# ScalarE's split of the next weight piece moved to the front of its half step

## The reference

```python
# layer 0
h = rms_norm(x, even_norm_g[i]);  proj = h @ even_w_in[i]         # q, k, v, z_a, u, z_b
q, k = rms_norm(q heads), rms_norm(k heads)                        # 8 heads of 128
o_a = stick_breaking_attention(q, k, v) * silu(z_a)                # exp(log_beta + rest)
o_b = s5_mixer(u, ...) * silu(z_b)                                 # state space, gelu, GLU
x = x + concatenate([o_a, o_b]) @ even_w_out[i]
# layer 1
proj = rms_norm(x, odd_norm_g[i]) @ odd_w_in[i]                    # q, k, v, z, r
o = gla_chunked(q, k, v, log_sigmoid(r @ gla_w_gate + gla_b_gate) / 16)
x = x + (rms_norm(o, gla_o_norm_g[i]) * silu(z)) @ odd_w_out[i]
# layers 2 and 3 (hybrid_layer)
h = rmsnorm(x, norm_w) * (1 + scale) + shift                       # shift, scale, gate: c_act @ w_ada + b_ada
qa, ka, va, za, qr, kr, vr, zr, ga, gr = split(h @ w_in)
s = qs @ kk * Dh ** -0.5;  m = max(s);  p = exp(s - m)             # 3 windows x 4 heads
y_att = merged windows of (p @ vv / sum(p)) * silu(za)
y_ret = retention(rotary(qr), rotary(kr), vr) * silu(zr)
merged = sigmoid(ga) * (y_att @ w_proj_attn) + sigmoid(gr) * (y_ret @ w_proj_ret)
x = x + gate * (merged @ w_out)
```

## Time and profile before

| | |
|---|---|
| median of 3 runs | 1077.22 us (1075.8 to 1077.54) |
| profiled execution | 1076.03 us |
| its span | 1074.2 us |
| TensorE busy | 1021.6 us, 95% |
| TensorE weight loads | 900.2 us, 84% |
| DVE busy | 704.9 us, 66% |
| ScalarE busy | 565.3 us, 53% |
| GpSimd busy | 336.5 us, 31% |
| granted clock of TensorE, mean | 0.987 |

### The profile page before, as it was taken

One profiled execution on the slowest core, in us unless ns is written; L12 is line 12 of the kernel. 1 busy time (PEld: TensorE's weight loads), 2 busy tenths in 40 slices (PEclk: granted clock), 3 DMA queues, 4 the chain that ended last, 5 costly groups with the idle time before them and its releaser, 6 DMA issues.

```text
span 1074.2 us, 15495 instructions
## 1 busy us (share of the span) xinstructions
PE 1021.6 (95%) x6084; PEld 900.2 (84%) x6084; DVE 704.9 (66%) x1072; ACT 565.3 (53%) x872; POOL 336.5 (31%) x349
## 2 busy tenths in 40 slices
PE   5999999989999799999999989979999999999995
PEld 5778889878968689998899868868999888998884
DVE  7894856888767664455576686774544565667665
ACT  5978577557344754455443344455444555334552
POOL 4700150433530173552453545321744000320001
PEclk9999999999999999999999989999999999999998
DMA  8543424767736487765565556745877436644531
GB/s 277 154 141 101 141 93 140 251 206 246 216 113 215 145 266 217 241 200 153 177 214 178 164 170 206 225 128 177 249 216 216 122 118 177 185 148 147 187 137 59
DMA packets 94440, 191.12 MB, mean 178 GB/s; under 512 B 6768, under 2 KB 10096, under 8 KB 94368
## 3 DMA queue, kind: packets, MB, share of 16 engines
q1 hardware_dynamic: 86256, 164.71, 49.6%
q0 software_dynamic: 6960, 22.71, 6.8%
q10 hardware_dynamic: 1152, 2.72, 0.7%
HBM read 189.07 MB, written 1.05 MB: 177 GB/s over the span
## 4 chain that ended last, share of the span: by engine, by line
PE 86%; DVE 6%; ACT 5%; DMA 1%; issue 1%; DVEq 0%; SPq 0%; ACTq 0%
PE G L593 15%; PE G L595 14%; PE G L594 14%; PE G L602 8%; PE G L604 8%; PE G L605 8%; PE B L556 2%; DVE WL L1526 1%; ACT AR L1046 1%; ACT WH L1046 1%; PE G L631 1%; PE G L633 1%; PE G L632 1%; DMA RAW<-in_even_w_in 1%; PE B L905 1%
## 5 line engine op out<-in xcount | busy, mean ns | idle before, releaser
L1526 DVE TENSOR_TENSOR WL<-RAW,WH 128x1024 fp32r<-128x1024 f32 (+2 forms) x306 | 398.5, 1306 | 258.2 <-ACT WH L1046 257.4
L1046 ACT ACTIVATE WH<-RAW 128x1024 fp32r<-128x1024 f32 (+2 forms) x306 | 320.2, 1050 | 282.9 <-PE G L595 142.7
L593 PE MATMUL G<-WH,HTh 128*128 128x512 f32 (+1 forms) x564 | 227.7, 404 | 2.8 <-DVE WL L1526 2.5
L602 PE MATMUL G<-HTh,WH 128*128 128x256 f32 x768 | 220.2, 287 | 0.5 <-DVE HTl L1602 0.5
L595 PE MATMUL G<-WL,HTh 128*128 128x512 f32 (+1 forms) x564 | 218.7, 388 | 0.0
L604 PE MATMUL G<-HTl,WH 128*128 128x256 f32 x768 | 217.9, 284 | 0.0
L605 PE MATMUL G<-HTh,WL 128*128 128x256 f32 x768 | 217.8, 284 | 0.0
L594 PE MATMUL G<-WH,HTl 128*128 128x512 f32 (+1 forms) x564 | 217.8, 386 | 0.0
L602 PEld LDWEIGHTS G<-HTh,WH 128*128 128x128 f32 x768 | 147.1, 191 | 2.4 <-issue 2.2
L604 PEld LDWEIGHTS G<-HTl,WH 128*128 128x128 f32 x768 | 147.1, 191 | 0.9 <-issue 0.7
L605 PEld LDWEIGHTS G<-HTh,WL 128*128 128x128 f32 x768 | 147.0, 191 | 0.0
(11 more groups left out here) (344 smaller groups left out, 1343.9 us busy)
## 6 DMA issues: line engine op xcount, KB each, us to landing
RAW<-in_w_in SPq DMA_DIRECT2D x176, 512.0 KB, 3.8
RAW<-in_even_w_in SPq DMA_DIRECT2D x40, 512.0 KB, 3.7
AR<-in_w_ada POOLq DMA_DIRECT2D x80, 256.0 KB, 3.9
RAW<-in_odd_w_in SPq DMA_DIRECT2D x16, 512.0 KB, 4.9
RAW<-in_w_proj_ret SPq DMA_DIRECT2D x16, 512.0 KB, 3.5
RAW<-in_w_out SPq DMA_DIRECT2D x16, 512.0 KB, 4.2
RAW<-in_even_w_out SPq DMA_DIRECT2D x12, 512.0 KB, 3.9
AR<-in_w_ada SPq DMA_DIRECT2D x16, 256.0 KB, 4.3
```

The lines of the kernel that those rows point to most:

```text
L593: nc.tensor.matmul(o, xh, wh, start=begins, stop=False)
L602: nc.tensor.matmul(o, fh, h_[:, kx, :], start=begins and f % 2 == 0, stop=False, skip_group_check=True)
L1046: return nc.scalar.activation(out_, ps, ACT.Copy, **kw)
L1526: vt(wl, raw, wh.bitcast(F32), ALU.subtract).then_inc(*dve.mark(LO, n))
```

## The change

In the three loops, the lines `if time % 2: hi((time + 1) // 2 + AHEAD)` go from the end of the body to its start. At each odd half step ScalarE so issues the split of the next piece, with its two waits (piece landed, piece n - 4 read), ahead of the copies, exponentials and other work of the same half step, in place of behind them. At even half steps nothing changes, and nothing on another engine does. Which instructions there are, their sizes and their buffers are the same.

```diff
--- before.py
+++ after.py
@@ -1381,6 +1381,8 @@
             nc.scalar.activation(er, er, ACT.Exp).then_inc(*act.mark(S5_A, "er"))
 
             for time in range(2 * groups["zr"]["at"] - 6):
+                if time % 2:
+                    hi((time + 1) // 2 + AHEAD)
                 if time in ENDS:
                     evac0(ENDS[time])
                 if time == 1:
@@ -1432,11 +1434,11 @@
                     act.wait_ge(*tile("glu", 1))
                     copy(YTh[:, 8 + 2 * i:10 + 2 * i, :], GY[:, 2 * i:2 * i + 2, :]).then_inc(
                         *act.mark(YT_HI, "glu", 2 * i))
+            next_layer(1)
+
+            for time in range(2 * groups["zr"]["at"], 2 * H0[0] - 6):
                 if time % 2:
                     hi((time + 1) // 2 + AHEAD)
-            next_layer(1)
-
-            for time in range(2 * groups["zr"]["at"], 2 * H0[0] - 6):
                 if time in ENDS:
                     evac1(ENDS[time])
                 if time == AT_GLA["rank"]:
@@ -1456,8 +1458,6 @@
                     h = AT_GLA["turn"][time]
                     act.wait_ge(*GO.of("g"))
                     yt_hi_scaled(YTh, 2 * h, lambda j: go[:, j:j + 1], "gla", h)
-                if time % 2:
-                    hi((time + 1) // 2 + AHEAD)
             act.wait_ge(*side("ada", 0, 3))
             nc.scalar.dma_start(ATM, const("attmask").rearrange("p (a b) -> p a b", a=2)).then_inc(l_atm, 16)
             nc.scalar.dma_start(DEC, const("decay").rearrange("p (a b) -> p a b", a=4)).then_inc(l_dec, 16)
@@ -1469,6 +1469,8 @@
                 act.wait_ge(*GNH_V.of(l))
                 for step in range(210):
                     time = 2 * H0[l] + step
+                    if step % 2 and (time + 1) // 2 + AHEAD < NP:
+                        hi((time + 1) // 2 + AHEAD)
                     if time in ENDS:
                         evac2(ENDS[time])
                     if l == 0 and step == AT_ANGLE["sin"]:
@@ -1500,8 +1502,6 @@
                     if step in AT_MRG:
                         c = 2 * AT_MRG.index(step)
                         yt_hi_scaled(YTh if c < 4 else HTh, c, lambda j: co["half"], "mrg", l, c)
-                    if step % 2 and (time + 1) // 2 + AHEAD < NP:
-                        hi((time + 1) // 2 + AHEAD)
             for ti in range(2):
                 for n in range(2):
                     square(3, ti, n)
```

## The result

| | before | after |
|---|---|---|
| median | 1076.68 us (4 runs, 1075.8 to 1077.54) | 1087.68 us (4 runs, 1085.61 to 1090.43) |
| ratio | | 1.0104, 95% interval 1.0084 to 1.0124 |
| profiled execution | 1076.03 us, span 1074.2 | 1086.81 us, span 1085.0 |
| mean granted clock of TensorE in it | 0.987 | 0.983 |

The kernel is 11.0 us slower. The forecast was 1089, 12.3 over the median of these runs of before, with a range of 1082.5 to 1094.

The account below looks back on a forecast made before the run. TensorE was taken to bound the kernel. 2.3 up to k0, 1.1 at half step 36 and 4.2 + 2.7 in attention made 10.3, with the clock 12.0, so 1089 us; range 1082.5 to 1094.

Parts of the forecast that it names:

- What bounds: Whole kernel: TensorE, busy 1021.6 of 1074.2 us, bounds it; only its waits can be won or added.
- The gain: Whole kernel: a split half is waited for only once, 2.5 us, all an earlier split can give back directly.
- the faster rival: Wait at split 11: its 2.5 us goes and nothing replaces it, giving 1074.7 us; chance 0.03.
- Up to k0: Layer 0, 24 to 62 us: ScalarE's copy of k0 comes late, eating the gain at split 11; +2.31 us.
- the first sign: At 50.9 us in the profile after: TensorE's wait for split 11's DVE half is near 0.
- Half step 36: Layer 0, fourth stick-breaking head: ScalarE's copies empty a bank late for the scores; +1.1 us (0 to 1.5).
- Attention: Layers 2 and 3: splits delay exponentials and copies past TensorE's use; +4.2 us in the first layer, +2.7 in the second.
- By head: First attention layer: heads 0 to 2 late by 1.6, 0.3 and 1.16 us, head 3's products by 1.1.
- the 3.0: Head 0, first attention layer: its lateness in us if the skill's table-load drain of about 1380 ns also counted.
- The clock: Behind k0's turn: the longer wait brings 3.4 us at half clock, +1.7 us, with a chance of 6 in 10.
- the rival's 1087.5: Behind k0, at 60 us: the clock holds, so the kernel takes 1087.5 us; chance 0.35.
- What costs nothing: Other ScalarE steps, retention, merge and layer openings: readers several half steps behind or order kept, so no cost.

Follow-up runs that it names:

- gla_only: Before, with the split moved to the front only in the second loop (layer 1): 1077.18 us, ratio 0.9999.
- one_split: Before, with only split 11 (half step 15) moved to the front, ahead of the sums of q0: 1077.48 us, ratio 1.0011.
- spread_late: Before, split behind as before, with the last of four spreads of u moved from half step 14 to 28: 1073.86 us, ratio 0.9973.
- layer0_only: Before, with the split moved to the front only in the first loop (layer 0): 1083.73 us, ratio 1.0055.
- table_tanh: After, with a table set holding both exp and tanh loaded at step 74 of layer 2, ahead of step 75's split: 1089.3 us, ratio 1.0113.
- attention_back: After, with the split set behind again at steps 75, 79, 81, 87, 93 and 95 of layers 2 and 3: 1082.94 us, ratio 1.0051.
- table_early: After, with the exponential's table (the logarithms' set) loaded at step 74 of layer 2, ahead of step 75's split: 1088.3 us, ratio 1.0097.
- hybrid_only: Before, with the split moved to the front only in the third loop (layers 2 and 3): 1082.18 us, ratio 1.0048.
- k0_twice: Before, with ScalarE doing the eight squares for the sums of k0 twice, no split moved: 1080.79 us, ratio 1.0043.
- late_part: Before, with the split in front only in layer 0 from half step 25 on: 1077.62 us, ratio 1.0006.

## Why the prediction was right

- **What bounds.** TensorE's waits, not ScalarE's idle time, give the time: +127 us of idling ahead of the splits cost 10.3 us of TensorE's waits. `gla_only` shows that idle time alone costs nothing.
- **The gain.** A split half was waited for once, and `one_split` shows that its 2.5 us can't be had by order: the faster rival (a chance of 0.03) is out, since ScalarE's sum of work ends at k0 in either order; `spread_late` shows the other side, as less work in that sum does win it.
- **Up to k0: +2.31 forecast, +1.95 in the traces.** The replay of ScalarE's list gave the place of each wait: 0.3, 1.3, 1.8 and 3.6 forecast at pieces 11, 12, 13 and k0. The trace has 1.20 and 1.57 for two pieces and 3.43. So the first sign (a wait near 0 at 50.9) failed in after, where TensorE came to split 11 1.1 us sooner than in before, as the half clock of the start had ended 2.5 sooner. Where it ended later (18.5, for 16.6 in after and 19.1 in before), the pattern is the one forecast: 0.35, 0.74, 1.60 and 3.41 in `layer0_only`. `one_split`, which has the same order at split 11, shows 0.42, 1.13, 1.61. The 0.36 between 2.31 and 1.95 is small and not taken apart.
- **Half step 36: +1.1 forecast, 1.08 of wait and 1.25 in the starts.** The three-bank circle was read rightly.
- **Attention: 4.2 and 2.7 forecast, 4.3 and 2.8 in the traces.** By head: 1.6, 0.3, 1.16 and 1.1 against steps of 1.5, 0.3, 1.2 and 1.25. The table load in the open is shown by `table_tanh`. Head 0 fits with the load's 1.28 alone: the wait is 1.43. (The prediction's own rows give 1.4 to 1.5 for it, not 1.6.) The Trainium skill (ScalarE: Activation LUTs, What ACT_TABLE_LOAD costs) adds a drain of about 1380 ns; the exponential starts 1.30 after the start of the load, so that no drain of that size shows here, and the 3.0 that I had worked out by it would have been too much.
- **The clock: +1.7 forecast, the term that was mis-sized.** I gave one stretch of 3.4 us at half clock to the wait ahead of k0, and 6 in 10 that it comes. The price of a stretch was right, the number wasn't: after has two, which cost 1.4 and 1.7. All five traces with after's order of work up to k0 have half clock there: 3.1 in after, 4.8 in `layer0_only`, 5.9 in `attention_back`, 4.8 in `table_early`, 5.7 in `table_tanh`. Elsewhere half clock moved as well, at the start (-1.1) and at the openings, which the prediction put at nothing, and all of it comes to 0.3 net in the pair of traces. So 1.7 was too little for the place and too much for the whole: the sum without it, 10.3, lies nearer to the 11.0 measured than the 12.0 with it. That this term did the forecast no harm is luck. The time fell next to the rival's 1087.5, in which the clock holds, and in the trace it didn't hold; other stretches made up for it. How much of half clock the other three executions of after have behind k0 isn't known.
- **What costs nothing.** Layer 1, the retention, the merge and the openings showed no new wait of TensorE on ScalarE, as forecast. Steps 77, 83 and 89 do cost something of their own (1.07 per layer in `attention_back`), which doesn't show in after, where larger waits stand ahead of them. The prediction had not looked at those.
- **Left open.** `hybrid_only` is 5.3 slower where its trace shows 7.1, with a clock that is 0.0025 higher in the mean. That the moved work changes where the openings fall against the clock is argued, not shown.

## What to carry to other kernels

An engine that does its list in order should not be made to wait for the bound engine ahead of work that this engine needs: here each split waits until TensorE has left its buffer, so it belongs behind everything of its half step that can run before. Read the price from the slack of the next reader at each place, two half steps here, and not from the engine's share of idle time; then look for what sets the sum of the list up to the next meeting point. Taking 2.7 us of work out of that stretch won what the order of the stretch could not.

## What the runs showed of the hardware

TensorE's clock made the runs of one kernel differ by more than I had expected: executions of `k0_twice` fall in two groups 5.4 us apart (medians of 1079.8 and 1085.2) at mean clocks of 0.982 to 0.986 and 0.978 to 0.979. Behind a wait of 3.4 to 3.5 us of TensorE ahead of k0, followed by few large matmuls and S5's small ones of 32 columns, six traces of six have 6.8 to 13.7 us at 0.50. The same matmuls ran at 1.00 behind a wait of 1.90 in before, but partly at 0.50 behind 2.08 in `one_split` and behind 0.65 in `late_part`. Half clock isn't always paid for: in `hybrid_only` 6.8 us of it behind a wait of 3.65 at split 11 used up the next wait (0 ahead of k0, for 1.90 in before), and k0 was turned only 0.5 us later than in before. A table load takes 1.28 us in every trace, hidden or not; where it was in the open, the next ACTIVATE started 1.30 us after the start of the load.
